# Placing the split weights, the experts' slots and the scatter's matrix 64 bytes off a multiple of 128 bytes

## What is computed

```
def swiglu_ffn(h, w_in, w_out):                    # 4 times; D_FF = 2816
    gate, up = jnp.split(h @ w_in, 2, axis=-1)
    return (jax.nn.silu(gate) * up) @ w_out

xm, z = jnp.split(h @ w_in, 2, axis=-1)            # mLSTM in-projection, 1024 x 4096
... = jnp.split(h @ w_in[l], IN_OFFSETS, axis=-1)  # mixer in-projection, twice
merged = (g[:, :, 0] * (y_a @ w_branch[l, 0]) + g[:, :, 1] * (y_b @ w_branch[l, 1])
          + g[:, :, 2] * (y_c @ w_branch[l, 2]))
x = x + merged @ w_out[l]

def expert_block(args):                            # mixture of experts, twice
    xb, e = args
    return (jax.nn.silu(xb @ w_gate[e]) * (xb @ w_up[e])) @ w_down[e]
```

## Time and profile before

| what | us |
|---|---|
| median of 3 runs | 2382.25 (2381.68 to 2383.2) |
| the profiled execution, first to last instruction (its span) | 2376.0 |
| the median less this span | 6.25 |
| PE matmuls busy in the span | 2259.9 (95%) |
| PE weight loads busy | 1731.4 (73%) |
| DVE, ACT, POOL busy | 1252.6, 948.1, 113.8 |

### The profile page before, as it was taken

One profiled execution on the slowest core, in us unless ns is written; L12 is line 12 of the kernel. 1 busy time (PEld: TensorE's weight loads), 2 busy tenths in 40 slices (PEclk: granted clock), 3 DMA queues, 4 the chain that ended last, 5 costly groups with the idle time before them and its releaser, 6 DMA issues.

```text
span 2376.0 us, 33274 instructions
## 1 busy us (share of the span) xinstructions
PE 2259.9 (95%) x12878; PEld 1731.4 (73%) x12878; DVE 1252.6 (53%) x2287; ACT 948.1 (40%) x1699; POOL 113.8 (5%) x96
## 2 busy tenths in 40 slices
PE   5999999998999899889999999999999999999999
PEld 3877784543577444468888689888788896798887
DVE  4624544111323411167755566777677636666776
ACT  2532212110322311164544664645554446655543
POOL 1000000000000000000024200000000052000000
PEclk9999999999999999999999999999999999999999
DMA  9976469999713899956654325466566535154663
GB/s 356 318 234 235 159 253 382 429 429 423 277 71 123 374 429 429 419 180 190 193 173 160 107 88 188 140 206 185 159 193 193 183 109 177 47 198 120 204 186 96
DMA packets 310253, 535.63 MB, mean 225 GB/s; under 512 B 14894, under 2 KB 200944, under 8 KB 296304
## 3 DMA queue, kind: packets, MB, share of 16 engines
q1 hardware_dynamic: 309180, 532.61, 62.2%
q10 hardware_dynamic: 948, 1.28, 0.2%
HBM read 532.81 MB, written 1.05 MB: 225 GB/s over the span
## 4 chain that ended last, share of the span: by engine, by line
PE 85%; DVE 7%; ACT 3%; issue 2%; DMA 2%; SPq 1%; POOL 0%; POOLq 0%; ACTq 0%; DVEq 0%
PE bank L601 15%; PE bank L1070 14%; PE bank L892 13%; PE yacc L930 9%; PE bank L897 7%; PE bank L585 5%; PE yacc L807 2%; PE yacc L618 2%; PE bank L636 2%; PE bank L1010 1%; PE bank L1285 1%; PE yacc L1082 1%; PE bank L672 1%; PE yacc L1229 1%; PE bank L766 1%
## 5 line engine op out<-in xcount | busy, mean ns | idle before, releaser
L1453 ACT ACTIVATE arena<-bank 128x256 f32<-128x256 f32 (+3 forms) x382 | 146.6, 407 | 575.3 <-PE bank L601 122.4
L892 PE MATMUL bank<-h_split,w_hi 128*128 128x512 f32 x1408 | 352.1, 392 | 0.0
L2366 DVE TENSOR_TENSOR w_lo<-wring,w_hi 128x1024 fp32r<-128x1024 f32 x264 | 307.5, 1218 | 3.3 <-ACT w_hi L1678 3.3
L1678 ACT ACTIVATE w_hi<-wring 128x1024 fp32r<-128x1024 f32 x264 | 277.6, 1056 | 48.4 <-PE yacc L930 48.2
L892 PEld LDWEIGHTS bank<-h_split,w_hi 128*128 128x128 f32 x1408 | 259.2, 189 | 50.0
L897 PEld LDWEIGHTS bank<-h_split,w_lo 128*128 128x128 f32 x1408 | 193.6, 191 | 20.5 <-issue 4.0
L897 PE MATMUL bank<-h_split,w_lo 128*128 128x256 f32 x1408 | 201.8, 285 | 3.8 <-ACT h_split L1587 3.6
L2976 POOL TENSOR_TENSOR wx_lo<-wring,wx_hi 128x1024 fp32r<-128x1024 f32 x42 | 107.3, 2557 | 1894.7 <-ACT wx_hi L1493 1894.7
L1070 PE MATMUL bank<-wring,arena 128*64 128x512 f32 x768 | 172.3, 603 | 12.2 <-issue 8.3
L1070 PE MATMUL bank<-arena 128*64 128x512 f32 x672 | 168.3, 594 | 10.6 <-issue 7.0
L1690 ACT ACTIVATE H<-bank 128x256 f32<-128x256 f32 x176 | 67.3, 383 | 250.9 <-PE bank L897 250.9
(11 more groups left out here) (412 smaller groups left out, 3793.9 us busy)
## 6 DMA issues: line engine op xcount, KB each, us to landing
wring<-in_ffn_w_in SPq DMA_DIRECT2D x176, 512.0 KB
wring<-in_w_ada SPq DMA_DIRECT2D x24, 2048.0 KB
wring<-in_ffn_w_out SPq DMA_DIRECT2D x88, 512.0 KB
wring<-in_w_in SPq DMA_DIRECT2D x20, 2048.0 KB
wring<-in_moe_w_down SPq DMA_DIRECT2D x16, 2048.0 KB, 23.2
wring<-in_moe_w_gate SPq DMA_DIRECT2D x16, 2048.0 KB, 18.1
wring<-in_moe_w_up SPq DMA_DIRECT2D x16, 2048.0 KB, 22.6
arena<-in_moe_w_gate SPq DMA_DIRECT2D x12, 2048.0 KB, 14.3
```

What stands on the lines that cost most here:

```text
L892: return mm(b[:, :], r(w_hi[:, j % 2, g, c * HB:(c + 1) * HB]), r(h_split[:, c, :, :].rearrange("p a t -> p (a t)")), start=start, stop=st ...
L1453: ins = f(dst, bank_of(name)[0:dst.shape[0], 0:T] if src is None else src, func, **kw)
L1678: f(w_hi[:, j % 2, part, :].bitcast(F32R), wring[:, u % WSLOTS, part * DC * HB:(part + 1) * DC * HB], ACT.Copy).then_inc(w_hi_ready[part], 1)
L2366: tt(w_lo[:, j % 2, part, :].bitcast(F32R), wring[:, (u0 + j) % WSLOTS, part * DC * HB:(part + 1) * DC * HB], w_hi[:, j % 2, part, :], ALU ...
```

## The change

Spacer tiles of 16 float32 (64 bytes) and larger numbers move tiles in SBUF. No instruction is added, removed or moved in its engine's order, and no size changes.

```
-MOE_EXTRA = (10496, 14592, 6400)
+MOE_EXTRA = (10512, 14608, 6416)
+HALF_LINES = 16
...
+        sb("before_s", [P, HALF_LINES])
         with nc.sbuf_tensor("S_pair", [P, TT, T], F32) as S_pair:
             pass
         neg_st = sb("neg_st", [P, TT, T])
+        sb("behind_s", [P, HALF_LINES])
...
-            part("before_w", [P, 8216 - 7168])
+            part("before_w", [P, 8240 - 7168])
             wt_merge = [part(name, [P, WBUFS, DC * P]) for name in ("wm_hi", "wm_lo")]
         with ExitStack() as overlay:
+            part("before_x", [P, HALF_LINES])
             wt_mix = [part(name, [P, 2, DC * P]) for name in ("wx_hi", "wx_lo")]
         with ExitStack() as overlay:
             part("before_w_in", [P, 12336])
             wt_w_in = [part(name, [P, WBUFS, DC * P]) for name in ("wi_hi", "wi_lo")]
+        sb("before_w_hi", [P, HALF_LINES])
         w_hi = sb("w_hi", [P, 2, 3, DC * HB])
         w_lo = sb("w_lo", [P, 2, 3, DC * HB])
+        sb("before_h_split", [P, HALF_LINES])
         h_split = sb("h_split", [P, DC, 2, T])
...
-        slot_g = view(6144, TT, 2, SLOTS)
+        slot_g = view(6160, TT, 2, SLOTS)
...
-        xb = view(4096, 8, PAD + T)
-        xv = view(6168, 8, T)
-        us = view(8216, 4, T)
+        xb = view(4120, 8, PAD + T)
+        xv = view(6192, 8, T)
+        us = view(8240, 4, T)
```

More of the change, by code:

```diff
@@ L506, in build @@
         yA, yB, yC = (view(1024 * i, 4, T) for i in range(3))
-        zs = view(10264, 4, T)
-        xb = view(4096, 8, PAD + T)
-        xv = view(6168, 8, T)
-        us = view(8216, 4, T)
-        vn = view(9240, TT, GMW)
-        cq = view(10264, 3, T)
-        ckv = view(11032, 2, T)
-        krs = view(11544, TT, ROPE)
-        wT = view(11608, GMG, P)
-        Vt = view(12120, TT, MH * MV)
-        O2 = 12760 + 384
+        zs = view(10288, 4, T)
+        xb = view(4120, 8, PAD + T)
+        xv = view(6192, 8, T)
+        us = view(8240, 4, T)
+        vn = view(9264, TT, GMW)
+        cq = view(10288, 3, T)
+        ckv = view(11056, 2, T)
+        krs = view(11568, TT, ROPE)
+        wT = view(11632, GMG, P)
+        Vt = view(12144, TT, MH * MV)
+        O2 = 12784 + 384
         Qt = view(O2, TT, MH, QK)
```

## The result

The changed kernel takes 2388.62 us (median of 5 runs, 2382.92 to 2389.89). The kernel before, run beside it, takes 2381.68 us (5 runs, 2376.31 to 2383.2). The ratio is 1.0035 with a 95% interval of 1.0025 to 1.0046: the change makes the kernel about 7 us slower. The forecast was 31 us faster, and the time lies above the top of the range (2374). The profiled execution has a span of 2381.1 us at a mean granted clock of 0.984, before 2376.0 at 0.986.

What follows compares the result with a forecast made beforehand. PE was taken to bound the kernel except in the DMA-bound experts' stages. Gains of 19.7 (feed-forward), 3.9, 5.4 and 1.9 us sum to 30.9, giving span 2345.1 and median 2351.4 us; range 2338 to 2374.

Steps and rivals of the forecast that it cites:

- What bounds the kernel: Whole kernel: PE busy 95% of the span and 85% of the path; shorter matmuls shorten all but the DMA-bound experts' stages.
- The trace of before already holds the experiment: Line 601: weights 64, 96 and 0 bytes off a multiple of 128 have medians 276, 280 and 282 ns, so offset matters.
- Line 897: Feed-forward, 256 columns: weights going from 0 to 64 bring matmuls from 120 to 114.9 ns, 5.1 ns gained each.
- Line 892: Feed-forward, 512 columns: the 13 ns excess seems paid once per weight load, so 5.1 ns gained each here too.
- Line 930: Feed-forward, 1056 matmuls, hidden tile stationary, weights moving at 64: 5.1 ns gained each, bounds -6.6 and +5 ns.
- Mixers' in-projection: 1008 matmuls in the mixers go from 118.8 to 114.9 ns, 3.9 us gained.
- Merge: 1728 matmuls on line 601 go from 118.0 to 114.9 ns, the mean of quick and slow patterns; 5.4 us gained.
- Out-product: 192 matmuls on line 618 go from 233.3 to 223.2 ns, 1.9 us gained.
- Experts' slots and the splitting: DMA writes into slots at 64, and DVE and ACT splitting into tiles at 64, cost nothing on the path: 0.
- The rule that speaks against it: Skill pages: independent SBUF read ports and 16-byte access lines mean nothing changes; time stays 2382.
- B: Rival: only 256-column matmuls gain, moving weights lose 5.0 ns on line 930; 11.2 us faster, 2371; partial gains 0.21.
- C: Rival: all 512-column feed-forward matmuls rise to line 618's 233.3 ns; 3.3 us slower, 2385.6; chance 0.04.

Runs made afterwards that it cites:

- m1_pairs: TensorE bench without the model, timing pairs of stationary and moving tiles at different addresses; 256 columns: 283 ns for 0 on 0, 276 for 64 on 0.
- m2_distance: Same bench without the model, 16 stationary tiles 32 bytes apart; medians at distances 0 and 64: 256 columns 284 and 276 ns, 512 columns 390 and 394.
- low_up_64: Kernel before with only the low parts of the feed-forward's gate and up weights at distance 64 from `h_split`; 2381.2 us, ratio 1.0003.
- l601_only: Kernel before with only `wx`, `wm` and the mixer's arena views moved, `wi` kept at distance 64; 2377.55 us, ratio 0.9997.

## Why the prediction was wrong

- **What bounds the kernel** held: PE stays on 85% of the path, the losses of its matmuls in the feed-forward show one for one, the float32 lines stayed, and the DMA rate stayed within 1%.
- **"The trace of before already holds the experiment"** was the step that failed first. I had three tiles on one line and ordered them by their own address modulo 128: 64, 96, 0. m1_pairs and m2_distance show that it is the distance to the moving operand, modulo 256. The true distances were 64, 224 and 128. The three numbers fitted both readings. Because of this I held `wi` to be untouched, when the 128 bytes ahead of the arena took it from 64 to 192: +2.1 to 2.4 us, where the sum had nothing. And I put the feed-forward's new distance at 64 when it was 192.
- **Line 897**, 5.1 ns each: 3.6 were measured in the quicker rhythm and 1.3 in the slower (the median, 283 to 279, mixes them). At 192 the table allows 3 to 4. And a true 64 would not have given more: low_up_64 has 117.8 ns between starts, 1.3 less than before, since in this stream the slow pattern stays.
- **Line 892**, 5.1 ns "paid once for each weight load": wrong in sign. The excess over the columns is about the same for both widths, and from this I concluded that the same shift would remove it. It is smallest at 0 for 512 columns. Line 899 lost 1.6 ns in the quicker rhythm and 3.6 in the slower (medians 392 and 394 in the two profiles, before 389).
- **Line 930** with "the roles exchanged": the same error, and the largest. Exchanging the roles turns 192 into 64, which is not the same distance, and for 512 columns 64 is worse. It lost 4.0 to 4.3 ns by the distance between starts (5 by the median of two of its three products), near the bound of 5 that I had taken from line 618. That row stood at a distance of 32 and not at an offset of 96. With the terms above the feed-forward comes to +3.2 to 4.1 us instead of -19.7.
- **Mixers' in-projection**, -3.9: the distance between starts fell as forecast (119.1 to about 115.3 ns), but not all of it showed in the stage, which I had taken for granted. It shortened by 0.9 us in the second mixer, and in the first by 0.7 in one profile, while it grew by 1.1 in the other, with a stretch at the lower clock.
- **Merge**, -5.4: one of four merges ran quickly (-3.1), the others not (+0.1), at the same addresses. A mean of the two patterns was a guess about which is caught, and here it was mostly the slow one.
- **Out-product**, 1.9: the medians went from 395 and 396 to 394, at most 0.4 us.
- **Experts' slots and the splitting**, 0: right within the scatter.
- **The rule that speaks against it.** The Trainium skill says in "TensorE: Matmul & The Clock Gate", "Step-by-step: what each phase is for", that the weight load and the running matmul read SBUF through ports of their own. I was right not to follow it to "no effect": m1_pairs has 276 and 283 ns by addresses alone.
- **The rivals.** B had the moving weights' loss about right (5.0 ns for 4.0 to 4.3). C, at 2385.6, had the sign, and its mechanism is the nearest: all 512-column matmuls lose. That its number is near is partly luck. It charged 12.6 us for them, where the distances measured come to 7 to 8, and it credited 9.3 us on line 601, where `wx` and `wm` gave 4.4 in one profile and cost 0.6 in the other, and `wi`, which it left out, took 2. I gave it 0.04 because I trusted a half-aligned 96 to lie between 0 and 64. For 512 columns the table has 390 at 0, 394 at 64 and 397 at 96, and nothing in between is certain.

No layout here beat the kernel before by more than the scatter. The best was l601_only at 0.9997.

## To carry to other kernels

For each stream of `fp32r` matmuls, write down the address of the stationary less that of the moving operand modulo 256, in both kernels, before you believe that an address does or does not change; a spacer moves every tile behind it. Measure the distance at the width in question, since 256 and 512 columns want different ones here, and with the neighbours that the stream has, since it keeps the timing in which it begins. Compare means of the distance between starts, since a median jumps when a stream has two patterns. The whole effect is 7 ns in 120 and 7 in 227, and stretches at the lower clock scatter by as much as a stage can gain.

## What was not expected of the hardware

- An `fp32r` matmul's pitch, the distance from its start to the next, depends on the distance of its operands modulo 256 bytes: 113 to 121 ns for 256 columns, 226 to 234 for 512, and the order of the distances differs between the widths.
- Distance 64 and distance 192 are not the same (276 and 280 ns; 394 and 392), so exchanging the operands is a change.
- A stream of 256 columns keeps 117.8 ns for 48 matmuls behind a run of 512 columns, in 31 of 32 groups, and has 113 with the same tiles by itself.
- At a distance of 64 every burst from rest is quick (16 of 16), at 192 two of 20 are. A whole feed-forward after the change runs its steps in 8.34 or in 8.41 us at the same addresses.
- The same program, with the same addresses, runs a whole merge in 80.98 or in 84.14 us, as the chain of the first profile after the change shows for its two merges:

```profile
1401.67 80.98 PE bank L608 x712
...
2068.45 84.14 PE bank L608 x712
```

- Time at the 1.2 GHz level went from 64.7 to 72.4 us between two profiles of the kernel before, and up to 88.1 in an experiment. A stretch of 3.4 us costs 1.7, which is a quarter of the 7 us that were to be explained.
